# Softmax heads in pairs: value products in plain fp32 at two places of the array, turned blocks copied once

## The chip, the cores and the metric

One NeuronCore of a Trainium2 chip runs the whole program. The metric is the device time of one execution in microseconds (us). Engines are named as in the profile: PE (matrix multiply; PEld its weight loads), DVE (vector), ACT (activation), POOL (GpSimd) and SP (which only starts DMAs here). Each works through its own instructions in order and waits on semaphores for the others.

## What is computed

A decoder trunk of two layers over 1024 tokens of width 1024, all in float32. Layer 0 mixes tokens by stick-breaking attention, layer 1 by latent attention (12 heads in 6 pairs, 96 wide for queries and keys, 64 wide for values, causal). In each layer 4 memory heads attend to 256 memory rows without a mask. The change touches the softmax heads only, which compute, head by head:

```python
sc = jnp.einsum('bhqd,bhkd->bhqk', q_blk, k).astype(jnp.float32) * scale
sc = jnp.where(key_pos <= q_pos, sc, -jnp.inf)      # latent heads only
p = jax.nn.softmax(sc, axis=-1)
o = jnp.einsum('bhqk,bhkd->bhqd', p.astype(v.dtype), v)
```

## The kernel before, in words

The program runs in stages: memory heads, stick-breaking, output projection with SwiGLU, and the same again for layer 1 with latent_inputs and latent_heads in the place of stick-breaking. The matrices are multiplied as float32r, a form of fp32 that PE takes in one pass with rounded operands. To keep precision an operand is split into a rounded upper part (hi, made by ACT) and the rest (lo, made by DVE or POOL), and two or three products are added up (`product3`, L82 to L84).

**Attend** (from L764) is the softmax attention of both the memory heads and the latent heads. A job is one head and one half of the queries (512 of them, four tiles of 128). Its steps are written into one list that all engines walk:

- S: the scores of one tile of 128 queries into one of two score buffers (PE), and the negated maximum of the rows (DVE, L931). S waits until the exponentials of the tile two before are done.
- P: the exponentials with their sum (ACT, L906). I and R: the reciprocal and the scaling of the rows (DVE, L937, L943).
- T: one block of 128 keys is turned by up to four transposes into a bank (PE, L882), which ACT copies as the upper part (L914) and from which DVE subtracts it for the lower (L948).
- V: the value product of the block turned one T earlier. The stationary operand `self.values(h, j)` is 128 wide: 64 columns of the upper and 64 of the lower part of the values. It is multiplied with the upper (L891) and the lower part (L893) of the turned block, so the bank holds two halves of 64 partitions.
- E: ACT copies the second half (L920), DVE adds the first (L954), and SP stores 64 x 512 numbers.
- X: extra work that the caller puts at certain places.

A causal job of half 0 has 4 blocks of 512, 384, 256 and 128 columns; one of half 1 has four of 512 and then the same four, 8 in all. The list has one slot for each T. In a slot the order is: missing R and I, T, V of the block before (and E), P, S as far as `plan` says, X as `extras` says.

**latent_heads** runs a loop of 5 turns over pairs of heads, between a prologue and a last pair (`closing`, without extras and without the next pair's scores). A turn attends for pair g and prepares pair g+1 by extras, all through one bank (7): eight projections ("project", each 24 matmuls), their statistics ("sum", "root", "normalise", "rotate" on ACT, DVE and POOL), the hi and lo parts of the weights after ("next weights": ACT; `lower_weights`: POOL, L2126), the split of the values (ACT L2192 and L2203, POOL L2121), and eight "turn" steps (four transposes of queries or keys, L2297; ACT upper part, L2196; DVE lower part, L2254). The order on POOL is written out by hand in `prepare`: `rotate(0)`, `lower_weights`, `rotate(1)`, `lower_values(0)`. DVE's "rotate" step waits for two products of POOL (rot_pool) before it overwrites their input.

Of the kernel before, what the change touches and what calls it, by code (L numbers as in the profile page):

```python
# [6 lines left out]
P = 128  # L7
F32 = mybir.dt.float32
F32R = mybir.dt.float32r
# [758 lines left out]
class Attend:  # L768
# [4 lines left out]

    def __init__(self, nc, ctx, tag, mem, psum, k, jobs, keys_of, blocks_of, causal, scores, values, store,
                 rows_mem, ring, score_banks, out_banks=(6, 7), plan=None, extras={}):
        self.nc, self.k, self.jobs, self.causal, self.ring = nc, k, jobs, causal, ring
        self.keys_of, self.blocks_of, self.scores, self.values, self.store = keys_of, blocks_of, scores, values, store  # L780
        self.p = [[rows_mem(f"{tag}_p{n}_{i}", [P, keys_of(4 * jobs[n][1] + i)]) for i in range(4)] for n in range(ring)]
        self.pt_hi = [mem(f"{tag}_pt_hi{s}", [P, HALF], F32R) for s in range(2)]
        self.pt_lo = [mem(f"{tag}_pt_lo{s}", [P, HALF], F32R) for s in range(2)]
        self.nmx, self.rsum, self.rinv = (mem(f"{tag}_{n}", [P, 4]) for n in ("nmx", "rsum", "rinv"))
        self.o_tmp = mem(f"{tag}_o_tmp", [HD, HALF])
        self.o_out = [mem(f"{tag}_o_out{s}", [HD, HALF]) for s in range(2)]
# [3 lines left out]
        (self.scores_made, self.nmax_done, self.exp_done, self.inv_done, self.rows_done,  # L790
         self.turned, self.hi_done, self.split_done, self.pv_made, self.tmp_done, self.out_done) = (
            ctx.semaphore(f"{tag}_{n}") for n in (
                "scores_made", "nmax_done", "exp_done", "inv_done", "rows_done", "turned",
                "hi_done", "split_done", "pv_made", "tmp_done", "out_done"))
        self.stored = [ctx.semaphore(f"{tag}_stored{s}") for s in range(2)]
        self.ns, self.nj = 4 * len(jobs), len(jobs)
        self.first = [sum(blocks_of(half) for _, half in jobs[:n]) for n in range(len(jobs) + 1)]
        self.nt = self.first[-1]

        if plan is None:
            plan = [6] + [min(self.ns, 4 * n + 6 + 4 * (j + 1) // blocks_of(half)) for n, (h, half) in enumerate(jobs)
                          for j in range(blocks_of(half))]
# [33 lines left out]
        for n in range(self.nj):  # L839
            blocks = blocks_of(jobs[n][1])  # L840
            for j in range(blocks):
                tau = self.first[n] + j
                row_up_to(max(rows, 4 * n + 4))
                inverse_up_to(exps - 1)
                steps.append(("T", n, j, tau))
                if tau:
                    steps.append(("V",) + self.of(tau - 1))
                    if j == 0:
                        steps.append(("E", n - 1))
                exp_up_to(made)  # L850
                score_up_to(plan[tau + 1])
                steps += [("X", x) for x in extras.get(tau, ())]
        steps += [("V",) + self.of(self.nt - 1), ("E", self.nj - 1)]
        row_up_to(plan[-1])
        self.steps = steps

        self.closing = [s for s in steps if s[0] not in "SPIR" or s[1] < self.nj]

    def of(self, tau):

        n = max(m for m in range(self.nj) if self.first[m] <= tau)
        return n, tau - self.first[n], tau

    def columns(self, n, j):

        return max(0, j - 4 * self.jobs[n][1]) * P if self.causal else 0

    def pe(self, pe, steps, turn=0, extra=None):
        for kind, *step in steps:
            if kind == "S":  # L870
                n, i = step
                s, (h, half) = 4 * n + i, self.jobs[n % self.nj]
# [3 lines left out]
            elif kind == "T":  # L876
                n, j, tau = step
                pe.wait_ge(self.rows_done, turn * self.ns + 4 * n + 4)
                if tau >= 2:
                    pe.wait_ge(self.split_done, turn * self.nt + tau - 1)  # L880
                for i in range(self.columns(n, j) // P, 4):
                    last = pe.transpose(self.t_ps[tau % 2][:, i * P:(i + 1) * P],  # L882
                                        self.p[n % self.ring][i][:, j * P:(j + 1) * P], self.k["ident"][:])
                last.then_inc(self.turned, 1)
            elif kind == "V":
                n, j, tau = step
                c0, h, o = self.columns(n, j), self.jobs[n][0], self.o_ps[n % len(self.o_ps)]
                pe.wait_ge(self.split_done, turn * self.nt + tau + 1)
                if j == 0:
                    pe.wait_ge(self.out_done, 1 + turn * self.nj + max(n + 1 - len(self.o_ps), 0))  # L890
                pe.matmul(o[:, c0:HALF], self.values(h, j), self.pt_hi[tau % 2][:, c0:HALF],  # L891
                          start=j == 0, stop=False, skip_group_check=True)
                pe.matmul(o[:, c0:HALF], self.values(h, j), self.pt_lo[tau % 2][:, c0:HALF], start=False,  # L893
                          stop=tau + 1 == self.first[n + 1], skip_group_check=True).then_inc(self.pv_made, 1)
            elif kind == "X" and extra:
                extra(pe, step[0], turn)

# [61 lines left out]
    def begin(self, sp):  # L959

        for s in (self.pv_made, self.out_done):
            sp.sem_inc(s, 1)
# [1432 lines left out]
```

## Time and profile before

| what | us |
|---|---|
| runs | 3103.78, 3103.95, 3100.43 (median 3103.78) |
| profiled execution | 3095.97 |
| its span | 3094.2 |
| PE busy in it | 2708.3 |
| stretch of the memory heads' attention, layer 0 and layer 1 | about 113 to 160, 1580 to 1628 |
| latent_heads: prologue, five loop turns, last pair | 1784 to 1849, 1849 to 2219.6, to 2279 |

A row of a group of instructions has busy time and mean duration, then the idle time before it and what ended that. In a timeline a row is one instruction or a run of them; the bracket is the idle time just before it. The start of a matmul is recorded, its end is modelled, so how long a matmul holds the array is read from the distance between starts.

### The profile page before, as it was taken

Reading aid. Unit: us, or ns where it says so; the run is one execution under the profiler, and the core shown is the slowest. Engines: PE = TensorE matmul, PEld = TensorE weight load, DVE = VectorE, ACT = ScalarE, POOL = GpSimd, SP = SyncE. Lnnn points to the kernel's source line nnn. Section 1 sums busy time; section 2 is a strip of 40 time slices with the busy share of each in tenths; the row PEclk is TensorE's granted clock in tenths of the full one; section 3 lists DMA queues with packets and bytes.
Section 4 is the critical chain, followed back from the end, with each engine's and each line's share of the span. In section 5 each row is a group of like instructions: output and inputs, shape, how many; then the busy total and the mean of one; then the engine's idle time right before and its main releaser. Section 6 shows DMA issues by size and latency. Waiting matters only on the chain. (4 is left out here: it accounts for less than half of the span.)

```text
span 3094.2 us, 40579 instructions
## 1 busy us (share of the span) xinstructions
PE 2708.3 (88%) x13104; PEld 2239.9 (72%) x13104; DVE 1479.6 (48%) x2548; ACT 1296.6 (42%) x2794; POOL 1036.7 (34%) x722
## 2 busy tenths in 40 slices
PE   5679999879899998999567668888879899998999
PEld 4567777657688886888547657777757688886887
DVE  5636666652855553111562236666643755553111
ACT  4435555652433332222442236666643433332222
POOL 2034445550544442444102011111120544443443
PEclk9899999999999999999788868999989899999999
DMA  3020000042222223454202000000041222223454
GB/s 110 11 65 28 28 27 27 7 147 92 69 81 82 83 82 133 143 170 138 67 11 60 12 23 6 20 22 24 7 170 68 82 81 81 81 81 123 151 171 139
DMA packets 143097, 232.38 MB, mean 75 GB/s; under 512 B 17056, under 2 KB 93856, under 8 KB 143008
## 3 DMA queue, kind: packets, MB, share of 16 engines
q1 hardware_dynamic: 143008, 231.24, 22.5%
q8 instruction: 50, 0.82, 0.1%
q14 instruction: 39, 0.32, 0.0%
HBM read 182.98 MB, written 48.23 MB: 75 GB/s over the span
## 5 line engine op out<-in xcount | busy, mean ns | idle before, releaser
L1485 POOL TENSOR_TENSOR l0s_run_lo<-l0s_run,l0s_run_hi 128x512 fp32r<-128x512 f32 (+3 forms) x144 | 177.4, 1232 | 219.2 <-DVE l0s_run_hi L1652 218.5
L363 POOL TENSOR_TENSOR l1f_dn_lo<-l1f_dn_raw,l1f_dn_hi 128x1024 fp32r<-128x1024 f32 x44 | 106.1, 2412 | 141.9 <-ACT l1f_dn_hi L428 141.9
L363 POOL TENSOR_TENSOR l0f_dn_lo<-l0f_dn_raw,l0f_dn_hi 128x1024 fp32r<-128x1024 f32 x44 | 105.7, 2403 | 140.3 <-ACT l0f_dn_hi L428 140.3
L82 PE MATMUL banks<-ht_hi,l0s_w_hi 128*128 128x512 f32 x288 | 140.3, 487 | 12.7 <-POOL l0s_w_lo L1475 12.7
L82 PE MATMUL banks<-l1f_dn_hi,l1f_a_hi 128*128 128x512 f32 x352 | 138.0, 392 | 15.3 <-issue 12.6
L82 PE MATMUL banks<-l0f_dn_hi,l0f_a_hi 128*128 128x512 f32 x352 | 138.2, 393 | 12.7 <-issue 11.8
L82 PE MATMUL banks<-l1f_T_hi,l1f_op_hi 128*128 128x512 f32 x352 | 139.6, 397 | 10.1 <-ACT l1f_b L444 5.3
L82 PE MATMUL banks<-l0f_T_hi,l0f_op_hi 128*128 128x512 f32 x352 | 139.1, 395 | 10.1 <-ACT l0f_b L444 5.3
L1642 DVE SCALAR_TENSOR_TENSOR l0s_run<-banks,l0s_soft 128x512 f32<-128x512 f32 (+3 forms) x144 | 80.2, 557 | 135.8 <-ACT l0s_soft L1543 134.7
L84 PE MATMUL banks<-l1f_T_hi,l1f_op_lo 128*128 128x512 f32 x352 | 139.3, 396 | 0.0
L83 PE MATMUL banks<-l1f_T_lo,l1f_op_hi 128*128 128x512 f32 x352 | 139.1, 395 | 0.0
L84 PE MATMUL banks<-l0f_T_hi,l0f_op_lo 128*128 128x512 f32 x352 | 138.9, 395 | 0.0
L83 PE MATMUL banks<-l0f_T_lo,l0f_op_hi 128*128 128x512 f32 x352 | 138.5, 394 | 0.0
L83 PE MATMUL banks<-l0f_dn_lo,l0f_a_hi 128*128 128x512 f32 x352 | 138.0, 392 | 0.0
L84 PE MATMUL banks<-l0f_dn_hi,l0f_a_lo 128*128 128x512 f32 x352 | 137.8, 391 | 0.0
L83 PE MATMUL banks<-l1f_dn_lo,l1f_a_hi 128*128 128x512 f32 x352 | 137.6, 391 | 0.0
L84 PE MATMUL banks<-l1f_dn_hi,l1f_a_lo 128*128 128x512 f32 x352 | 137.5, 391 | 0.0
L948 DVE TENSOR_TENSOR l1aa_pt_lo<-banks,l1aa_pt_hi 128x512 fp32r<-128x512 f32 (+2 forms) x144 | 79.3, 550 | 116.1 <-ACT l1aa_pt_hi L914 115.9
L589 DVE TENSOR_TENSOR l1f_a_lo<-l1f_a_raw,l1f_a_hi 128x512 fp32r<-128x512 f32 x44 | 33.9, 770 | 208.0 <-ACT l1f_a_hi L426 208.0
L1514 ACT ACTIVATE l0s_soft<-banks 128x512 f32<-128x512 f32 (+3 forms) x144 | 70.9, 492 | 147.6 <-PE banks L1710 101.5
L589 DVE TENSOR_TENSOR l0f_a_lo<-l0f_a_raw,l0f_a_hi 128x512 fp32r<-128x512 f32 x44 | 32.2, 732 | 207.7 <-ACT l0f_a_hi L426 207.7
L1758 PE MATMUL banks<-l0s_wt,l0s_v 128*128 128x512 f32 (+3 forms) x288 | 119.0, 495 | 9.3 <-DVE l0s_o_out L1663 7.5
(481 smaller groups left out, 8600.3 us busy)
## 6 DMA issues: line engine op xcount, KB each, us to landing
l0f_raw<-in_w_ffn_gu_dram SPq DMA_DIRECT2D x22, 1024.0 KB, 5.2
l0f_dn_raw<-in_w_ffn_down_dram SPq DMA_DIRECT2D x44, 512.0 KB, 3.9
l1f_raw<-in_w_ffn_gu_dram SPq DMA_DIRECT2D x22, 1024.0 KB, 5.2
l1f_dn_raw<-in_w_ffn_down_dram SPq DMA_DIRECT2D x44, 512.0 KB, 4.0
hidden_rows<-l0f_hid SPq DMA_DIRECT2D x22, 512.0 KB, 2.8
l0f_a_raw<-hidden_rows SPq DMA_DIRECT2D x44, 256.0 KB, 3.1
hidden_rows<-l1f_hid SPq DMA_DIRECT2D x22, 512.0 KB, 2.7
l1f_a_raw<-hidden_rows SPq DMA_DIRECT2D x44, 256.0 KB, 3.1
```

The costliest lines, as they stand in the source:

```text
L82: pe.matmul(out, l_hi, r_hi, start=first, stop=False, skip_group_check=True)
L83: pe.matmul(out, l_hi, r_lo, start=False, stop=False, skip_group_check=True)
L84: return pe.matmul(out, l_lo, r_hi, start=False, stop=last, skip_group_check=True)
L363: pool.tensor_tensor(dn_lo[e][:], dn_raw[e][:], as_f32(dn_hi[e][:]), ALU.subtract).then_inc(dn_lo_done, 1)
L589: dve.tensor_tensor(a_lo[e][:], a_raw[e][:], as_f32(a_hi[e][:]), ALU.subtract).then_inc(a_lo_done, 1)
L948: dve.tensor_tensor(self.pt_lo[tau % 2][:, c0:HALF], self.t_ps[tau % 2][:, c0:HALF], as_f32(self.pt_hi[tau % 2][:, c0:HALF]), ALU.subtract ...
L1485: pool.tensor_tensor(run_lo[t % NR][:, f:HALF], run[t % NR][:, f:HALF], as_f32(run_hi[t % NR][:, f:HALF]), ALU.subtract).then_inc(run_spli ...
L1514: act.activation(s[:, f:HALF], psum[b % NZ][:, f:HALF], ACT.Abs).then_inc(abs_done, 1)
L1642: dve.scalar_tensor_tensor(r[:, f:HALF], psum[t % NZ][:, f:HALF], 0.0, soft[t % NA][:, f:HALF], ALU.max, ALU.add).then_inc(sp_done, 1)
L1758: pe.matmul(out_bank[:, f:HALF], v[:, j, h, :], wt[b % NW][:, f:HALF], start=bb in START, stop=bb in END, skip_group_check=True).then_inc( ...
```

## The change

Heads go two at a time. A job is now a pair of heads and a half of the queries (2 instead of 4 jobs in latent_heads, 4 instead of 8 in the memory heads). There is one T per head and block as before (so as many slots: 24 a turn), but one V per pair and block, in the slot of the next block's first head. Both T are plain fp32: ACT copies head 0's block, DVE head 1's. The value product is one fp32 matmul per head, 64 stationary columns, to partitions 0 to 63 and 64 to 127 of one bank. DVE copies the 128 x 512 result once and SP stores it once. The values are no longer split: in the memory heads they are read from `k32`; in latent_heads POOL copies them by a multiplication with one (`copy_values`). Extras, plan and the order of the turns are new, and waits on the turns at the head of the loop become waits before each part's first scores (`ready`).

```diff
@@ Attend.__init__, the list of steps
-        for n in range(self.nj):
-            blocks = blocks_of(jobs[n][1])
-            for j in range(blocks):
-                tau = self.first[n] + j
-                row_up_to(max(rows, 4 * n + 4))
...
+        for m in range(self.nj):
+            for j in range(blocks_of(jobs[m][1])):
+                u = self.first[m] + j
+                for h in range(2):
+                    row_up_to(max(rows, 4 * (2 * m + h) + 4))
+                    inverse_up_to(exps - 1)
+                    steps.append(("T", m, j, h, u))
+                    if h == 0 and u:
+                        steps.append(("V",) + self.of(u - 1))
+                        if j == 0:
+                            steps.append(("E", m - 1))
+                    exp_up_to(made)
+                    score_up_to(plan[2 * u + h + 1])
+                    steps += [("X", x) for x in extras.get(2 * u + h, ())]
@@ Attend.pe, V
-                pe.matmul(o[:, c0:HALF], self.values(h, j), self.pt_hi[tau % 2][:, c0:HALF],
-                          start=j == 0, stop=False, skip_group_check=True)
-                pe.matmul(o[:, c0:HALF], self.values(h, j), self.pt_lo[tau % 2][:, c0:HALF], start=False,
-                          stop=tau + 1 == self.first[n + 1], skip_group_check=True).then_inc(self.pv_made, 1)
+                for h in range(2):
+                    pe.wait_ge(self.copied[h], turn * self.nu + u + 1)
...
+                for h in range(2):
+                    last = pe.matmul(o[h * HD:(h + 1) * HD, c0:HALF], self.values(2 * pair + h, j),
+                                     self.pt[u % 2][h][:, c0:HALF], start=j == 0, stop=u + 1 == self.first[m + 1],
+                                     skip_group_check=True)
+                last.then_inc(self.pv_made, 1)
@@ Attend.act and Attend.dve, T
+                act.activation(self.pt[u % 2][0][:, c0:HALF], self.t_ps[0][:, c0:HALF],
+                               ACT.Copy).then_inc(self.copied[0], 1)
+                dve.tensor_copy(self.pt[u % 2][1][:, c0:HALF], self.t_ps[1][:, c0:HALF]).then_inc(self.copied[1], 1)
@@ Attend.dve, E
-                dve.tensor_tensor(self.o_out[n % 2][:], self.o_ps[n % len(self.o_ps)][0:HD, :], self.o_tmp[:],
-                                  ALU.add).then_inc(self.out_done, 1)
+                dve.tensor_copy(self.o_out[m % 2][:], self.o_ps[m % len(self.o_ps)][:]).then_inc(self.out_done, 1)
@@ Attend.begin
+        sp.sem_inc(self.pv_made, self.nu)
@@ latent_heads
-    turns = [(a, h, half) for h in range(2) for half in range(2) for a in range(2)]
+    turns = [(a, h, half) for half in range(2) for h in range(2) for a in range(2)]
...
-    extras = {0: ["values 1", "project 0"], 1: ["project 1"], 2: ["project 2"], 3: ["project 3"],
-              4: ["project 4", "sum 0", "root 0"], 5: ["project 5", "normalise 0"], 6: ["project 6", "rotate 0"],
-              7: ["project 7"], 8: ["next weights", "sum 1", "root 1"], 9: ["normalise 1"],
-              10: ["rotate 1", "turn 0"], 11: ["used 1", "turn 1"], 12: ["turn 2"], 13: ["values 0", "turn 3"],
-              14: ["turn 4"], 16: ["turn 5"], 18: ["turn 6"], 21: ["turn 7"]}
-    plan = [8, 9, 10, 11, 12, 13, 13, 14, 14, 15, 15, 16, 16, 16, 17, 18, 19, 20, 20, 21, 21, 22, 22, 23, 24]
+    extras = {0: ["project 0"], 1: ["project 1"], 3: ["project 2"], 4: ["project 3"], 5: ["sum 0", "root 0"],
+              6: ["normalise 0", "project 4"], 7: ["rotate 0"], 8: ["project 5"], 9: ["turn 0"],
+              10: ["turn 1", "project 6"], 11: ["turn 2"], 12: ["turn 3", "project 7"],
+              13: ["next weights", "sum 1", "root 1"], 14: ["normalise 1"], 15: ["rotate 1"], 17: ["turn 4"],
+              18: ["turn 5"], 19: ["turn 6"], 20: ["turn 7"]}
+    plan = [8] + list(range(9, 17)) + [16] * 5 + list(range(17, 25)) + [24] * 3
...
+        def ready(pe, n, g):
+            pe.wait_ge(t_split, 1 + 8 * g + 2 * n + 2)
@@ POOL in latent_heads
-                pool.tensor_tensor(v[:, h, :, HD:], v_head(h), as_f32(v[:, h, :, 0:HD]), ALU.subtract).then_inc(v_split, 1)
+            def copy_values(n, g):
+                pool.wait_ge(evicted, 1 + NS * g + NS // 2 * (n + 1))
+                pool.wait_ge(at_.pv_made, at_.nu * g + (8, 12)[n])
+                pool.tensor_tensor(v[:, group(n), :], v32[:, group(n), :],
+                                   one[:].unsqueeze(2).broadcast_to([P, G // 2, HD]), ALU.mult).then_inc(v_copied, 1)
...
             def prepare(g):
                 rotate(0, g)
+                copy_values(0, g)
                 lower_weights(g + 1)
                 rotate(1, g)
-                lower_values(0, 2 * g)
+                copy_values(1, g)
```

## Rows read from the trace of the kernel before

**Rows 1.** The page, part 1: busy time, share of the span, instructions.

```profile
PE 2708.3 (88%) x13104; PEld 2239.9 (72%) x13104; DVE 1479.6 (48%) x2548; ACT 1296.6 (42%) x2794; POOL 1036.7 (34%) x722
```

**Rows 2.** Busy time by stretch: length, PE, PEld, DVE, ACT, POOL, clock, DMA.

```profile
112.00:160.00 48.00, 31.85 (x148) 21.99 (x148) 36.62 (x107) 27.49 (x80) 0.00 (x0) 0.89 0.10 21
...
1849.00:1923.30 74.30, 64.69 (x405) 58.61 (x404) 43.86 (x91) 49.79 (x161) 13.62 (x12) 0.84 0.03 7
...
2145.50:2219.60 74.10, 62.49 (x432) 55.46 (x432) 47.48 (x99) 52.00 (x167) 13.70 (x12) 0.98 0.07 19
2219.60:2279.00 59.40, 43.42 (x228) 34.55 (x228) 37.91 (x78) 28.36 (x62) 1.49 (x1) 0.91 0.05 11
```

**Rows 3.** Waits of PE, 1850 to 2280 us: total, times, longest.

```profile
PE banks L891 <- DVE l1aa_pt_lo L948: 44.0, 47, 3.4
PE banks L2297 <- DVE l1a_kt_lo L2254: 7.3, 8, 1.2
...
PE banks L891 <- DVE l1aa_o_out L954: 3.4, 3, 2.2
```

**Rows 4.** Waits of PE, last loop turn, 2143 to 2214 us.

```profile
PE banks L891 <- DVE l1aa_pt_lo L948: 7.2, 7, 3.4
```

**Rows 5.** Timeline of PE, last loop turn: start, duration, operation, idle before.

```profile
2192.96 0.39 PE L893 MATMUL banks<-l1aa_pt_lo,l1a_v 128*128 128x512 f32 x1
2193.19 0.39 PE L82 MATMUL banks<-l1a_kt_hi,l1a_qt_hi 96*128 96x512 f32 x1
...
2200.44 0.63 PE L82 MATMUL banks<-l1a_kt_hi,l1a_qt_hi 96*128 96x512 f32 x1
2200.87 0.63 PE L83 MATMUL banks<-l1a_kt_lo,l1a_qt_hi 96*128 96x512 f32 x1
...
2206.55 0.60 PE L882 MATMUL banks<-ident,l1aa_p 128*128 128x128 f32 x4
2206.91 0.31 PE L891 MATMUL banks<-l1aa_pt_hi,l1a_v 128*128 128x128 f32 x1
```

**Rows 6.** Timeline of PE in stick_breaking: one fp32 value product, 512 columns.

```profile
402.28 1.02 PE L1758 MATMUL banks<-l0s_wt,l0s_v 128*128 128x512 f32 x2
...
403.37 0.40 PE L83 MATMUL banks<-ht_lo,l0s_w_hi 128*128 128x512 f32 x1
```

**Rows 7.** Timeline of ACT after the last projection of a turn.

```profile
2192.49 0.33 ACT L2176 ACTIVATE l1a_q<-banks 128x192 f32<-128x192 f32 x1 [0.56 <-PE banks L84]
...
2196.39 1.28 ACT L2188 ACT_TABLE_LOAD   x1
...
2198.59 0.31 ACT L2188 ACTIVATE l1a_std<-l1a_ss,eps 128x16 f32<-128x16 f32 x1 [0.92 <-DVE l1a_ss L2232]
```

**Rows 8.** Timeline of POOL in the same turn.

```profile
2195.92 2.62 POOL L2126 TENSOR_TENSOR l1a_wq_lo<-l1a_wq_raw,l1a_wq_hi 128x1152 fp32r<-128x1152 f32 x1 [5.58 <-ACT l1a_wq_hi L2160]
2198.50 1.26 POOL L2126 TENSOR_TENSOR l1a_wk_lo<-l1a_wk_raw,l1a_wk_hi 128x512 fp32r<-128x512 f32 x1
2200.11 1.39 POOL L2131 TENSOR_TENSOR l1a_k<-k_rot,l1a_rstd 128x256 f32<-128x256 f32 x1 [0.35 <-DVE l1a_rstd L2236]
2201.46 0.90 POOL L2136 TENSOR_TENSOR l1a_rc<-l1a_q,rope_tab 128x128 f32<-128x128 f32 x1
2202.33 0.45 POOL L2137 TENSOR_TENSOR l1a_rd<-l1a_q,rope_tab 128x128 f32<-128x128 f32 x1
2205.11 0.49 POOL L2140 TENSOR_TENSOR l1a_q<-l1a_rc,l1a_rd 128x128 f32<-128x128 f32 x1 [2.33 <-DVE l1a_rb L2246]
```

**Rows 9.** Timeline: two turned blocks in a row through the one bank.

```profile
1824.21 1.09 PE L2297 MATMUL banks<-ident,l1a_q 128*96 128x128 f32 x4 [1.56 <-DVE l1a_kt_lo L2254]
```

**Rows 10.** Instruction groups, 105 to 160 us (memory heads, layer 0).

```profile
L948 DVE TENSOR_TENSOR l0ma_pt_lo<-banks,l0ma_pt_hi 128x512 fp32r<-128x512 f32 x16 | 11.1, 691 | 6.7 <-ACT l0ma_pt_hi L914 6.7
```

**Rows 11.** Instructions of lines 1663 and 2121: duration ns min/median/max.

```profile
L1663 DVE COPY l0s_o_out<-banks x12: 672/682/690, 270.3 to 656.4; 128x512 f32<-128x512 f32 x12
...
L2121 POOL TENSOR_TENSOR l1a_v<-l1a_v,l1a_v x12: 1315/1493/2010, 1820.7 to 2235.5; 128x512 fp32r<-128x512 f32 x12
```

More of the change, by code:

```diff
@@ L871, in pe @@
                 n, i = step
-                s, (h, half) = 4 * n + i, self.jobs[n % self.nj]
+                s, (h, half) = 4 * n + i, self.parts[n % self.np]
+                if i == 0 and self.ready:
+                    self.ready(pe, n, turn)
                 if s >= len(self.s_ps):
@@ L876, in pe @@
             elif kind == "T":
-                n, j, tau = step
+                m, j, h, u = step
+                n = 2 * m + h
                 pe.wait_ge(self.rows_done, turn * self.ns + 4 * n + 4)
[L879 to L882, printed above, removed]
+                if u:
+                    pe.wait_ge(self.copied[h], turn * self.nu + u)
@@ L883, in pe @@
+                for i in range(self.columns(m, j) // P, 4):
+                    last = pe.transpose(self.t_ps[h][:, i * P:(i + 1) * P],
                                         self.p[n % self.ring][i][:, j * P:(j + 1) * P], self.k["ident"][:])
-                last.then_inc(self.turned, 1)
+                last.then_inc(self.turned[h], 1)
             elif kind == "V":
-                n, j, tau = step
-                c0, h, o = self.columns(n, j), self.jobs[n][0], self.o_ps[n % len(self.o_ps)]
@@ L966, in sync @@
     def sync(self, sp, turn=0):
[L967 to L969 removed]
+        for m, (pair, half) in enumerate(self.jobs):
+            sp.wait_ge(self.out_done, 1 + turn * self.nj + m + 1)
+            sp.dma_start(self.store(pair, half, turn), self.o_out[m % 2][:]).then_inc(self.stored[m % 2], 16)
     def finish(self, sp, turns=1):
@@ L2073, in latent_heads @@
[L2073 to L2078 removed]
+        sem = lambda n: ctx.semaphore(f"{tag}_{n}")
@@ L2093, in _ @@
             at_.begin(sp)
-            for s in (made, evicted, squared, v_split, turned, t_split):
+            for s in (made, evicted, squared, t_split):
                 sp.sem_inc(s, 1)
+            sp.sem_inc(v_copied, 2)
+            sp.sem_inc(turned, 8)
             load(0)
@@ L2261, in _ @@
             with dve.Fori(0, PAIRS - 1) as g:
-                at_.dve(dve, at_.steps, g, lambda dve, step, g: step not in OWN and prepare(dve, step, g + 1))
+                at_.dve(dve, at_.steps, g, lambda dve, step, g: prepare(dve, step, g + 1))
             at_.dve(dve, at_.closing, PAIRS - 1)
```

218 lines of the change are left out of this document (92 added, 126 removed).

## The prediction

> **What bounds the kernel now.** I read the page's busy times first, then the busy times by stretch, then the waits of PE, then timelines. PE is busy 2708.3 of 3094.2 us [rows 1], but the change touches only three stretches, and each has its own limit.
>
> In a loop turn of the latent heads (five, 74.1 us each) PE is recorded busy 62.5 to 64.7 us, ACT 50 to 52, DVE 44 to 47 [rows 2]. PE is the limit, and its idle time is what an edit can win. Over all pairs it waits 44.0 us for the lower part of a turned block, 3.4 us for an output bank and, in the loop turns, two times about 7 us at the "turn" steps [rows 3]. The last turn alone has 7.2 us of waits of V, the longest 3.4 us [rows 4]. That one has a history: ACT, in order, first makes the next weights, loads a table (1.28 us), waits for DVE's sum and only then copies the block [rows 7]. After it PE runs for a while at half its clock, 1.2 and not 2.4 GHz: products of 512 columns start 0.43 us apart and not 0.23 [rows 5].
>
> In the last pair nothing but attention is left: 59.4 us, PE 43.4 busy, DVE 37.9 [rows 2]. The chain of scores, exponentials, turned block, hi, lo and product sets the pace. In the memory heads DVE is busy 36.6 of 48 us [rows 2], and its largest wait, 6.7 us, is for ACT's upper part [rows 10]: DVE and its partner bound that stretch.
>
> **The value products.** Before, a block of 512 columns costs two fp32r products of 0.23 us for each head [rows 5], so 0.93 us a pair. Summed over its blocks a head has 9 times 512 columns, which makes 8.4 us a turn. A plain fp32 product of 512 columns is recorded as two matmuls with a load each, and holds PE from 402.28 to about 403.14 (the second matmul after it starts at 403.37, and they run 0.23 apart): 0.86 us, two passes of 0.43 [rows 6]. No row shows two products at two column places. Bounds for a pair's block: 0.86 if both stream together, 1.72 if they don't. PE starts matmuls in order, here pass 1 and 2 of head 0, pass 1 and 2 of head 1. Pass 2 of a head needs its own place, pass 1 of the other head does not; so I take three steps of 0.43, the middle pair together: 1.29. A turn then costs 7.7, 11.6 or 15.5 us: -0.7, +3.2 or +7.1 (I take +3.2).
>
> By the Trainium skill, TensorEngine Tiling (Array Packing), "Theoretical Speedup" and "Key Properties", tiles work independently and two column tiles give up to twice the rate, but a change of tiling mode drains the engine. The first rule would make the pair 0.86 us and is a rival below; the second speaks against the change, since each V stands between full-width transposes and scores, two switches each, 24 a turn. No row here prices a switch, and the sum has none.
>
> **The waits of V.** The chain from a turned block to its product loses one of its two links: DVE's subtraction of 0.69 us behind ACT [rows 10], and head 0's copy has a slot to spare. Of the 7 us I leave 1. But the ACT backlog stays. From the start of the last eviction to the end of the root it needs 6.4 us (2192.49 to 2198.90), then it loads the table back (1.28) and makes the exponentials of score 16: some 8 us [rows 7]. PE has meanwhile the slots 13 to 15 up to score 18, which needs that buffer: three T at about 0.4 (0.36 to the next start [rows 5]), one V, two small S, about 3.3 us. So some 4.8 us of wait return at S. Net -1.4 us a turn.
>
> **POOL's queue, the term that decides.** `copy_values(0)` overwrites values that V 4 to 7 of the running pair read; it waits for pv_made of V 7. V 7 stands in slot 16. Behind it in POOL's queue stand `lower_weights` and `rotate(1)`. "rotate 1" is an extra of slot 15 on DVE and waits there for POOL's two products; "turn 4", slot 17 on PE, waits for the same chain. Before, the only wait on V in POOL's way was over in the turn's first slots ("values 1"): POOL goes from 2195.92 to 2202.8 through weights and rotation [rows 8], and PE never waited there. After V 7 POOL has: the copy, bounded by 1.3 and 2.0 from the subtraction of the same size [rows 11], taken as 1.4 since DVE stands still meanwhile; weights 2.62 + 1.26; rotation 1.39 + 0.90 + 0.45; the last addition 0.5 [rows 8]. Sum 8.5 us, 8.7 with hand-over. PE has in this time S 19 (three products of 0.23 and the mask, 0.76), T (0.4) and S 20 (0.4): 1.6. It stands still for 7.1 us. DVE stood too, so its maximum, rows and copy come late for V 8: 1 us more. Together +8.1. It can't be less than zero; at most, with the 2.01 copy, 9. PE's pause is longer than the one that ended at half clock, so I add 1 us for slow products behind it (a product of 512 columns loses 0.20 us there [rows 5]; I count five of them, in less dense work).
>
> **One bank, two uses in a slot.** Slots 10 and 12 hold a turn and a projection. A second use of bank 7 right behind a turn waits for ACT's and DVE's parts: 1.56 us [rows 9]. Two of these are 3.1 us, the other turns some 2, against the 3.0 now ((7.3 + 7.2) / 5, of which one row stands in [rows 3]). +2.1 us a turn.
>
> Loop turn: 3.2 - 1.4 + 8.1 + 1.0 + 2.1 = +13.0 us, times five = +65.
>
> **Last pair, prologue.** Without extras the POOL chain is gone. DVE and ACT lose about half their work on turned blocks. Of the 12.6 us of waits of V and bank there I take back some 60 percent and pay 1 to 3 for the products: -7 (between 0 and -12). In the prologue all eight turns stood behind "rotate 1"; now four go ahead of "project 7" (four times 2.65 us, 1.09 of transposes and 1.56 of wait [rows 9]) and four remain: +1. The values' split leaves ACT (1.3 us a turn) but PE isn't held by it: zero, covered by PE's own work; if that cover is gone it is a gain of at most 1 us a turn.
>
> **Memory heads.** For each pair and half DVE made four subtractions of 0.69 us and two additions about as long, and waited four times 0.4 for ACT (6.7 us over 16 [rows 10]). It now makes two block copies and one output copy of 0.68 (a copy from a bank is no cheaper than a subtraction [rows 11]). Three saved are 2.0 us, less some overlap 1.8, and waits 0.9: -2.7 for each of 4 units, in two layers, -21. Bounds: -26 if all DVE waits go, -12 if the products take 1.72 and hold up the scores. The dropped split of values: -1. The fewer and larger stores are nothing: SP is far from late; only the last store, some 2 us, is exposed as before.
>
> Sum: 65 - 7 + 1 - 21 - 1 = +37 us on the profiled execution's 3096.0, or 3133. The median of the runs is 7.8 us above it, so 3141 against 3103.8. A measurement of this kernel can tell about 0.2 percent, 6 us, from no change.
>
> **Rivals.**
> - **The two products stream wholly together.** 0.86 a block: 3.9 us a turn less (-19.5), memory -24, last pair -9: +12, 3116. For it: the places and banks allow it. Against: a product's two passes come before the other head's. Of this rival the Trainium skill's first rule above would be the reason. 14 percent.
> - **They don't overlap, so the change doesn't do what it says.** 1.72: +3.9 a turn (19.5), memory -14, last pair -4: +66, 3170. For it: every matmul in the trace starts only after the one before has streamed. 28 percent.
> - **POOL's wait is covered, and the shorter copy chain decides.** The place is slots 15 to 17: if ACT's backlog and late maxima hold PE back at score 18 as long as POOL needs, or V 7 comes earlier than I count, the 8.1 and 1.0 us of each turn go. 37 - 46 = -9, 3095; with products together 12 - 46 = -34, 3070. It decides once less than about 1 us of the 8.1 is left. Against: V 7 itself lies behind that backlog, so the two add up. 14 percent, around 3091.
> - My forecast has the remaining 44 percent, with its own range 3118 to 3160 from the bounds of last pair, memory heads and waits.
>
> Range: 3100 to 3178 leaves out most of the faster case and the upper edge of the serial one. Faster by over 0.2 percent only in the third rival (0.13); same where that one and the first meet (0.07); slower 0.80.
>
> **What would show it.** DVE's last subtraction of "rotate" waiting about 7 us for POOL once a turn, and PE's turn step after it idle as long; `copy_values` on POOL released by PE and followed without a gap by L2126's work; value products of a pair's block 1.29 us from first start to the next instruction; a loop turn of 87 us; the memory heads' stretch near 37 us. The forecast is wrong if a turn is under 76 us, or if POOL's copy starts when PE is not waiting soon after; serial if the next start is 1.72 behind.

## The result, and the profile after

The changed kernel takes 3137.0 us (median of 4 runs, 3133.2 to 3138.0) against 3103.9 for the kernel before, run beside it: a ratio of 1.0107, 95% interval 1.0089 to 1.0124. I forecast 3141, range 3100 to 3178. Each later group of runs had the kernel before beside it too (medians 3100.9 to 3103.6), so kernels are compared by their ratios; the changed kernel stands at 1.0107 x 3101 = 3134 on that scale.

The page, part 1, and the busy times by stretch (columns as in [rows 2]): the first layer's memory heads, two loop turns of the latent heads, and the latent prologue.

```profile
PE 2739.5 (87%) x13104; PEld 2217.7 (71%) x13104; DVE 1422.2 (45%) x2438; ACT 1226.6 (39%) x2652; POOL 1023.2 (33%) x723
```

```profile
105.00:153.30 48.30, 35.82 (x167) 21.70 (x165) 34.03 (x110) 23.11 (x74) 0.00 (x0) 0.85 0.05 17
1888.60:1973.80 85.20, 68.84 (x441) 53.81 (x440) 41.02 (x85) 44.26 (x154) 10.93 (x12) 0.90 0.05 17
2144.70:2230.00 85.30, 68.84 (x434) 53.90 (x434) 40.56 (x84) 43.63 (x150) 10.93 (x12) 0.90 0.05 16
...
1762.60:1840.80 78.20, 40.16 (x232) 35.70 (x232) 15.84 (x24) 24.34 (x104) 15.76 (x15) 0.67 0.12 33
```

DVE and ACT are relieved as intended (57 and 70 us over the whole run against [rows 1]), but PE is busy 31 us longer with the same 13104 matmuls. The five turns are best measured together, from the first transpose of the first pair's probabilities to that of the last pair. First before, then after:

```profile
1853.41 1.06 PE L882 MATMUL banks<-ident,l1aa_p 128*128 128x128 f32 x4
...
2231.79 0.62 PE L882 MATMUL banks<-ident,l1aa_p 128*128 128x128 f32 x4
```

```profile
1850.19 1.05 PE L875 MATMUL banks<-ident,l1aa_p 128*128 128x128 f32 x4
...
2278.29 0.66 PE L875 MATMUL banks<-ident,l1aa_p 128*128 128x128 f32 x4
```

Five turns: 378.4 before, 428.1 after, +49.7, or +9.9 a turn. (The 74.1 us from which I forecast was one turn of 73.8 to 77.8; the mean was 75.7.) PE's waits over all pairs after the change, to be read beside [rows 3]:

```profile
PE banks L2290 <- DVE l1a_q L2236: 23.4, 5, 5.5
PE banks L82 <- ACT l1aa_p L907: 22.1, 11, 3.8
PE banks L82 <- DVE l1a_kt_lo L2241: 15.6, 10, 1.6
PE banks L888 <- DVE l1aa_pt L943: 14.0, 20, 1.7
PE banks L875 <- DVE l1aa_p L938: 7.4, 6, 3.5
PE banks L2290 <- DVE l1a_kt_lo L2241: 3.0, 5, 0.6
PE banks L2290 <- DVE l1a_qt_lo L2241: 1.9, 5, 0.4
```

With two small ones that are not shown (1.3 and 1.1) these make 89.8 us; before, the rows of [rows 3] with one of 7.2 for turned blocks and two small ones made 63.1: +26.7. In the whole attention of the latent heads PE was busy 369.5 us and is now 385.6: +16.1. Together +42.8; that stretch grew from 436.6 to 478.7 us. So the waits of V fell (47.4 to 15.1), and three new ones cost more: turn 4 for the rotation, scores for exponentials, projections for the bank.

**The POOL chain** is there as forecast. POOL in the last loop turn:

```profile
2172.41 1.04 POOL L2118 TENSOR_TENSOR l1a_v<-l1a_v,l1a_one 128x512 f32<-128x512 f32 x1 [31.59 <-PE banks L888]
2173.41 2.62 POOL L2124 TENSOR_TENSOR l1a_wq_lo<-l1a_wq_raw,l1a_wq_hi 128x1152 fp32r<-128x1152 f32 x1
2175.99 1.26 POOL L2124 TENSOR_TENSOR l1a_wk_lo<-l1a_wk_raw,l1a_wk_hi 128x512 fp32r<-128x512 f32 x1
2177.21 0.61 POOL L2129 TENSOR_TENSOR l1a_k<-k_rot,l1a_rstd 128x256 f32<-128x256 f32 x1
```

And PE beside it, score 18 (waiting for ACT), V 7, and turn 4 (waiting for POOL's rotation through DVE):

```profile
2168.12 0.69 PE L82 MATMUL banks<-l1a_kt_hi,l1a_qt_hi 96*128 96x384 f32 x1 [3.63 <-ACT l1aa_p L907]
...
2170.34 1.98 PE L888 MATMUL banks<-l1aa_pt,l1a_v 128*64 128x512 f32 x4
...
2179.57 1.06 PE L2290 MATMUL banks<-ident,l1a_q 128*96 128x128 f32 x4 [4.35 <-DVE l1a_q L2236]
```

POOL stands idle for 31.59 us until V 7 is through, then copies, lowers the weights and rotates without a gap. DVE waits 8.2 us for it, PE 4.35.

### The profile page after: what moved, and what is told of

Same layout as the page of the kernel before. It is cut to its first block and busy times, and to the rows that moved or that the text cites. A ratio compares the mean times of both kernels' runs of the same rounds, so it can differ in the third digit from the quotient of the medians.

```text
span 3136.0 us, 40078 instructions
## 1 busy us (share of the span) xinstructions
PE 2739.5 (87%) x13104; PEld 2217.7 (71%) x13104; DVE 1422.2 (45%) x2438; ACT 1226.6 (39%) x2652; POOL 1023.2 (33%) x723
## 5 line engine op out<-in xcount | busy, mean ns | idle before, releaser
L82 PE MATMUL banks<-ht_hi,l0s_w_hi 128*128 128x512 f32 x288 | 141.2, 490 | 11.7 <-POOL l0s_w_lo L1463 11.7
L82 PE MATMUL banks<-l1f_dn_hi,l1f_a_hi 128*128 128x512 f32 x352 | 138.0, 392 | 14.1 <-issue 11.8
L358 POOL TENSOR_TENSOR l1f_hid<-l1f_c,l1f_gate 128x512 f32<-128x512 f32 x44 | 66.8, 1519 | 173.2 <-DVE l1f_c L550 173.2
```

Source lines behind the costliest of these rows:

```text
L82: pe.matmul(out, l_hi, r_hi, start=first, stop=False, skip_group_check=True)
L358: pool.tensor_tensor(hidden(q), cs[q][:], gate[q][:], ALU.mult).then_inc(hid_done, 1)
```

## The experiments

Twelve kernels ran; kernel 7, for example, is that of experiment 7. Ratios are to the kernel before.

**1. POOL's order.** On POOL alone:

```
-                copy_values(0, g)
                 lower_weights(g + 1)
                 rotate(1, g)
+                copy_values(0, g)
```

> The changed kernel with one edit: on POOL copy_values(0) stands behind rotate(1) and no longer ahead of lower_weights. My theory: the place of that copy, and nothing in the rotation itself, holds PE at turn 4 (4.4 us in the last turn). The wait of DVE's last rotate subtraction for POOL (8.2 us) falls under 2 us, PE's wait at turn 4 falls under 1 us, and the half-clock stretch behind it goes: a loop turn of 85.2 us becomes 78 to 81, the median 3137 becomes 3102 to 3115. Rival 1: another wait stands behind this one (ACT's backlog or the bank), turn 4 comes as late as before: within 5 us of 3137. Rival 2: only the 4.4 us of the row go and nothing with them: 3137 - 22 = 3115.

3100.1 us, 0.9996 (0.9987 to 1.0005), 2 us below my range: 34 us of the changed kernel's loss are gone, all that set it apart from the kernel before. DVE's wait for POOL and PE's at turn 4 have left the tables. PE's remaining waits over all pairs:

```profile
PE banks L82 <- ACT l1aa_p L907: 21.8, 11, 3.8
PE banks L82 <- DVE l1a_kt_lo L2241: 15.6, 10, 1.6
PE banks L888 <- DVE l1aa_pt L943: 14.0, 20, 1.7
PE banks L875 <- DVE l1aa_p L938: 7.5, 6, 3.5
```

Only the row of 23.4 us is missing; the others stand as they were. Yet 34 us went: PE's busy time over the pairs fell too, from 385.6 to 375.6, with the granted clock at 0.91 and not 0.89 of full. So the wait that POOL caused, 23.4 us, cost some 10 us more in slow products behind it. Both rivals fall.

**2 and 3. Do the two products run together?** Two kernels in which they can't, one with products over the full width of the array, one with both at one place of 64 columns. Both leave out the separation of the two heads' results; they serve for their times alone.

```
-                    last = pe.matmul(o[h * HD:(h + 1) * HD, c0:HALF], self.values(2 * pair + h, j),
...
+  full width:       last = pe.matmul(o[:, c0:HALF], v[:, 2 * j:2 * j + 2, :], ...
+  same place:       last = pe.matmul(o[0:HD, c0:HALF], self.values(2 * pair + h, j), ...
```

> The changed kernel, but in the latent heads each value product takes both heads' values (128 columns of the array) and writes the whole bank, so the two products can't stand side by side and there is no change of the array's shape. It leaves out the separation of the two heads. Theory A (side by side both products stream wholly together, and a block pays two changes of shape, 0.35 us): a pair's block of 512 columns costs 1.72 instead of 1.21, one of 128 columns 0.43 instead of 0.57; 15.5 us a turn instead of 11.9, six turns +21: 3158. Theory B (my prediction's three steps of 0.43, no price of a change of shape): every block a third dearer, 128 columns 0.43 instead of 0.32, 15.5 instead of 11.6: +23, 3160. The totals agree; the row of a 128-column block tells them apart. Theory C (they never ran together): no change, 3137.

> The changed kernel, but in the latent heads both heads' value products (64 columns each, as in the changed kernel) go to the same column place of the array and the same half of the bank. It leaves out the second head's own sum. Theory A (full overlap side by side, plus 0.35 us for two changes of shape): the overlap goes, the changes stay: 9 x 1.72 + 12 x 0.35 = 19.7 us a turn instead of 11.9, six turns +47: 3184. Theory B (three steps, a change of shape costs nothing): 15.5 instead of 11.6, +23: 3160, the same as the full-width kernel. Theory C (no overlap before): no change, 3137.

3144.9 us, 1.0140 (1.0124 to 1.0155), and 3164.5 us, 1.0219 (1.0195 to 1.0243): +10 and +35 us over the changed kernel. By their order they speak for theory A (B wants both alike, C neither dearer), but both are some 11 us short of its sums. The traces tell part of why. Three timelines of PE in the last pair, one block's products, the next eight transposes and the next block's products: the changed kernel, full width, same place.

```profile
2307.36 1.08 PE L888 MATMUL banks<-l1aa_pt,l1a_v 128*64 128x512 f32 x4 [0.44 <-DVE l1aa_pt L943]
2308.37 1.09 PE L875 MATMUL banks<-ident,l1aa_p 128*128 128x128 f32 x8
2309.90 0.65 PE L888 MATMUL banks<-l1aa_pt,l1a_v 128*64 128x512 f32 x2 [0.44 <-DVE l1aa_pt L943]
```

```profile
2307.04 1.96 PE L889 MATMUL banks<-l1aa_pt,l1a_v 128*128 128x512 f32 x4 [0.44 <-DVE l1aa_pt L944]
2308.83 1.04 PE L875 MATMUL banks<-ident,l1aa_p 128*128 128x128 f32 x8
2310.30 0.67 PE L889 MATMUL banks<-l1aa_pt,l1a_v 128*128 128x512 f32 x1 [0.44 <-DVE l1aa_pt L944]
```

```profile
2328.36 1.90 PE L889 MATMUL banks<-l1aa_pt,l1a_v 128*64 128x512 f32 x4 [0.44 <-DVE l1aa_pt L944]
...
2331.72 0.61 PE L889 MATMUL banks<-l1aa_pt,l1a_v 128*64 128x512 f32 x1 [0.44 <-DVE l1aa_pt L944]
```

All with the same idle 0.44 us in front, at the full clock. From block to block: 2.54, 3.26 and 3.36 us. Same place against full width, 0.10 us, I read as what going over to 64 columns and back costs; the two kernels differ besides only in the width of the weights loaded and of the output. Side by side against same place, 0.82 us, is the overlap: of two products of 0.86 us [rows 6] nearly one whole. The records say the same. In a block of the last loop turn the four matmuls start in two pairs (PE's timeline, two narrow windows):

```profile
2202.70 0.65 PE L888 MATMUL banks<-l1aa_pt,l1a_v 128*64 128x512 f32 x2
...
2203.18 0.60 PE L888 MATMUL banks<-l1aa_pt,l1a_v 128*64 128x512 f32 x2
```

The pairs start 0.48 apart. At one place no two of them start together (a block's four take 1.84 us to the next start in the third timeline, 0.46 each), so a pair is one matmul of each head: first passes together, then second passes. My expectations took 0.35 us for two changes of shape; that was the whole hand-over around a block, most of which a full-width product has too (1.79 us to the next start, of which two products stream 1.72).

With these prices full width should cost 9 x 0.82 - 12 x 0.10 = 6.2 us a turn, 37 in six turns, and same place 9 x 0.82 = 7.4, or 44. The runs gave 10 and 35. What is missing lies in PE's busy time (over the pairs 394.4 us with full width against 385.6, where the prices ask for 37 more), and with it in the clock. Windows of the third loop turn, of the same length and aligned on the turn's start, for full width, then the changed kernel, then same place:

```profile
2068.00:2089.00 21.00, 13.84 (x80) 9.94 (x78) 6.70 (x15) 10.49 (x27) 3.90 (x3) 1.00 0.00 0
```

```profile
2069.80:2090.80 21.00, 15.03 (x72) 11.41 (x72) 5.96 (x14) 9.29 (x25) 3.55 (x2) 0.76 0.00 0
```

```profile
2078.00:2099.00 21.00, 14.15 (x80) 9.11 (x78) 6.70 (x15) 10.06 (x27) 3.92 (x3) 1.00 0.00 0
```

With full-width products the granted clock stayed at 2.4 GHz (1.00) through the turn's first waits, where in the changed kernel it fell to 1.2 for a part (0.76). The waits are alike but not the same: two of 1.55 us before projections in each kernel, and at score 18 3.1 us with full width, 3.7 in the changed kernel, 3.0 at the same place. The third kernel shows that products of 64 columns are not by themselves what brings the clock down: with them, too, the window stands at 1.00, in this turn and the two after it, though not in the first two (0.84 in the second). What both kernels have in common is that the two heads' products follow each other. Why that left the clock higher stays open. Over the whole of the pairs the granted clock was 0.94 with full width, 0.91 at the same place and 0.89 in the changed kernel.

**4. The memory heads alone.** The changed memory heads with the latent heads of before (in code: the old Attend kept under another name for latent_heads).

> The kernel before with the change made in the two stretches of memory heads alone; the latent heads are those of before. My theory: what those stretches showed in the changed kernel is a gain of their own, 2 x 7.5 us, of which their prologues and the next stretch's start take back some 5: 3104 - 10 = 3094, ratio 0.997. Rival 1: the gain is wholly given back at the next stretch's start (a load or a first projection that is not earlier): 3104. Rival 2: it is the full 21 us of my prediction: 3083.

3086.7 us, 0.9952 (0.9938 to 0.9965): -15 us, between my theory and the full forecast. The part is a gain, and worth keeping alone. DVE's waits in the first layer's stretch of the changed kernel:

```profile
DVE l0ma_pt L943 <- PE banks L875: 5.3, 5, 3.2
DVE l0m_q_st L1194 <- PE banks L1279: 3.2, 2, 2.1
DVE l0ma_nmx L926 <- PE banks L1313: 2.8, 5, 1.6
DVE l0ma_o_out L948 <- PE banks L888: 2.5, 4, 1.3
```

The wait of 6.7 us for ACT [rows 10] is gone, but waits for PE took its place: in sum 13.0 us before, 14.9 now. The stretch went from 52.2 to 44.7 us, and DVE's busy time in it from 40.3 to 33.1: its saved instructions (4 x 2.0) came nearly in full, its saved waits didn't.

**5. The bank's second use.** The order of experiment 1, and the extras from slot 10 on spread out:

```
-              6: ["normalise 0", "project 4"], 7: ["rotate 0"], 8: ["project 5"], 9: ["turn 0"],
-              10: ["turn 1", "project 6"], 11: ["turn 2"], 12: ["turn 3", "project 7"],
-              13: ["next weights", "sum 1", "root 1"], 14: ["normalise 1"], 15: ["rotate 1"], 17: ["turn 4"],
-              18: ["turn 5"], 19: ["turn 6"], 20: ["turn 7"]}
+              6: ["normalise 0", "project 4"], 7: ["rotate 0"], 8: ["project 5"], 9: ["turn 0"], 10: ["turn 1"],
+              11: ["project 6"], 12: ["turn 2"], 13: ["turn 3"], 14: ["project 7"],
+              15: ["next weights", "sum 1", "root 1"], 16: ["normalise 1"], 17: ["rotate 1"], 19: ["turn 4"],
+              20: ["turn 5"], 21: ["turn 6"], 22: ["turn 7"]}
```

> The POOL order of the first experiment (3100), and the extras of the second half spread so that no slot holds a turn and a projection (project 6 in slot 11, turns 2 and 3 in 12 and 13, project 7 in 14, the rest one or two slots later). My theory: the 15.6 us that PE waits there ahead of projections for the lower part of a turned block (10 times 1.56) are paid because the second use stands right behind the first, and go: 3100 - 12 to 15 = 3085 to 3088, a loop turn near 75.5. Rival: the pace of that half is set by ACT's queue (evictions, exponentials), and the waits come up again at the scores: 3098 to 3102.

3105.1 us, 1.0013 (1.0004 to 1.0022): 5 us slower than experiment 1; my theory missed, and by more than the rival. Stretch of all pairs, experiment 1 and this one:

```profile
1836.40:2281.00 444.60, 375.64 (x2362) 293.32 (x2361) 235.62 (x483) 237.31 (x785) 60.84 (x60) 0.91 0.05 14
```

```profile
1833.50:2284.80 451.30, 383.75 (x2362) 301.51 (x2360) 235.77 (x483) 237.62 (x785) 62.22 (x60) 0.88 0.04 14
```

PE's waits sum to the same (65.7 and 64.9 us): 10 of the 15.6 us before projections went and came back at turns and scores. What grew is PE's busy time, by 8.1 us, with the clock at 0.88. Why these places suit the clock less I did not try.

**6. The prologue's order.** Experiment 1 with all projections ahead of all turns in the prologue, as before.

```
-                "project 4", "project 5", "turn 0", "turn 1", "project 6", "turn 2", "turn 3", "project 7",
-                "next weights", "sum 1", "root 1", "normalise 1", "rotate 1"] + [f"turn {n}" for n in range(4, 8)])
+                "project 4", "project 5", "project 6", "project 7", "next weights", "sum 1", "root 1", "normalise 1",
+                "rotate 1"] + [f"turn {n}" for n in range(8)])
```

> The POOL order of the first experiment (3100), and in the prologue of the latent heads alone the order of the kernel before (all projections, weights, second half of the rotation, then turns 0 to 7). My theory: the 6.4 us by which the prologue grew come from four turns in series ahead of project 7 and from projects 6 and 7 at half clock behind their waits, while turns 0 to 3 no longer stand behind a wait for the rotation anyway: from the first latent project to the first score 78.2 us becomes 72, the median 3094. Rival (my prediction's +1: the order costs almost nothing, the rest of the 6.4 lies in the earlier projects or loads): 77, 3099.

3093.1 us, 0.9972 (0.9963 to 0.9982): 7 us, as my theory said. The prologue's stretch is 71.8 us, as before, against 78.2. (These windows begin 11 us ahead of the first project; from that to the first score it is 58.7 against 65.1, the same 6.4.)

**7. Next weights later.** Kernel 5 with the edit below. The list for the prologue (`PREPARE`) gets the same order, "next weights" behind "rotate 1".

```
-              15: ["next weights", "sum 1", "root 1"], 16: ["normalise 1"], 17: ["rotate 1"], 19: ["turn 4"],
+              15: ["sum 1", "root 1"], 16: ["normalise 1"], 17: ["rotate 1"], 18: ["next weights"], 19: ["turn 4"],
...
-                lower_weights(g + 1)
                 rotate(1, g)
+                lower_weights(g + 1)
```

> The pooled and spread kernel, with next weights moved on ACT from slot 15 to slot 18, behind the root and the rotation, and lower_weights on POOL behind rotate(1). My theory: PE's wait of 3.8 us at score 18 is ACT's backlog (0.8 of copies and squares, 1.76 of upper weights, 1.28 table, 0.31 root, 0.58 block copy, 1.28 table), so taking 1.76 us out of it shortens it by as much in five turns, -9: 3077 to 3080. Rival: the wait is for DVE's sum and the tables, the weights fill time that ACT waits anyway: as the pooled and spread kernel, 3086.

3091.2 us, 0.9965 (0.9952 to 0.9979): -14 where -9 was expected; the time that I named, 3077 to 3080, started from 3086 for kernel 5 and so missed. PE's wait for exponentials fell from 24.3 to 16.4 us, near what I expected. The rest has two parts. PE's busy time over the pairs fell by 4.5 us (383.8 to 379.3) with the clock at 0.90 and not 0.88. And the edit reached the prologue, which my expectation left out: PE's wait at turn 4 there fell from 10.3 to 6.4 us, and from the first project to the first score it is 60.3 us and not 65.3.

**8. Opening scores first.** Experiment 7, and in the prologue turns 0 to 3 and the opening scores ahead of turns 4 to 7:

```
-            for step in PREPARE:
-                prepare(pe, step, 0)
+            for step in PREPARE[:20]:
+                prepare(pe, step, 0, BANK_USES[0])
             at_.pe(pe, at_.opening)
+            for step in PREPARE[20:]:
+                prepare(pe, step, 0, BANK_USES[0])
...
```

(PE's part; ACT and DVE walk the same order, and `PREPARE` is put into it.)

> The kernel with next weights late, and a prologue in which projections 4 to 7 stand together, turns 0 to 3 are made during the second half's rotation, and the opening scores, which need no more than turns 0 to 3, are made ahead of turns 4 to 7. My theory: the 10.3 us that PE waits at turn 4 in the prologue are filled, and projects 6 and 7 run at the full clock: -12 to -16 against the kernel with next weights late, so 3062 to 3067. Rival: the opening's exponentials and rows on ACT and DVE hold back the rotation and turns 4 to 7 by as much, only the order's 6 us come back: 3072.

3079.5 us, 0.9928 (0.9914 to 0.9942): -11.7 against kernel 7, just short of the 12 to 16 that I expected, and twice the rival's 6.

**9 and 10. Without the spreading.** Kernels 7 and 8 with the changed kernel's own slots (turn 1 with project 6, turn 3 with project 7), root in slot 13, next weights in 16:

```
...
+              10: ["turn 1", "project 6"], 11: ["turn 2"], 12: ["turn 3", "project 7"],
+              13: ["sum 1", "root 1"], 14: ["normalise 1"], 15: ["rotate 1"], 16: ["next weights"], 17: ["turn 4"],
...
```

> The slots of the changed kernel (turn 1 with project 6, turn 3 with project 7), the rotation first on POOL, and next weights on ACT at slot 16, behind the rotation. Theory A (the spread slots lost by the clock: they left PE's waits the same in sum, 65 us, and its granted clock at 0.88 of full and not 0.91): without the spreading the late weights give their 9 us (1.76 us of ACT ahead of score 18, five turns) on top of the first experiment's 3100, and the clock stays near 0.91: 3088 to 3092, no worse than the spread kernel with late weights (3091). Theory B (spreading was a gain that noise hid): 3096 to 3100.

> As the packed kernel with late weights, with the prologue that makes the opening scores ahead of turns 4 to 7. It gave 12 us in the spread kernel; if it adds, 3076 to 3080. Rival: the prologue's gain was that of the order of projections and turns alone (7 us): 3082 to 3085.

3096.2 us, 0.9980 (0.9970 to 0.9991), and 3081.8 us, 0.9931 (0.9912 to 0.9950). The first touches the lower edge of theory B's range, and its 12 runs reach from 3089 to 3102, over both ranges; it decides nothing between them. In its profiled execution the wait for exponentials is down from kernel 1's 21.8 us to 14.8, yet the way from the first transpose to the last product of the pairs is 434.4 us against 434.0: PE's busy time took the gain back (380.8 us in a stretch of 442.0, against 375.6 in 444.6). The second is 14 us below the first, so the opening adds here too, where the rival had 7; its time misses the 3076 to 3080 that I named, since it starts from 3096. It can't be told from kernel 8, and kernels 7 and 9 differ by 5 us with intervals that overlap. So spreading neither clearly wins nor clearly loses once the weights are late.

**11. Root early.** Kernel 10 with projects 6 and 7 in slots 9 and 10, sum and root in 11, normalise in 12, rotate in 13, while no score waits to be made:

```
-              6: ["normalise 0", "project 4"], 7: ["rotate 0"], 8: ["project 5"], 9: ["turn 0"],
-              10: ["turn 1", "project 6"], 11: ["turn 2"], 12: ["turn 3", "project 7"],
-              13: ["sum 1", "root 1"], 14: ["normalise 1"], 15: ["rotate 1"], 16: ["next weights"], 17: ["turn 4"],
+              6: ["normalise 0", "project 4"], 7: ["rotate 0"], 8: ["project 5"], 9: ["project 6"],
+              10: ["project 7"], 11: ["turn 0", "sum 1", "root 1"], 12: ["turn 1", "normalise 1"],
+              13: ["turn 2", "rotate 1"], 14: ["turn 3"], 16: ["next weights"], 17: ["turn 4"],
```

> As the packed kernel with the opening first, with projects 6 and 7 in slots 9 and 10, ahead of all turns, and sum 1 and root 1 in slot 11, normalise 1 in 12, rotate 1 in 13. Theory A (what PE waits for at score 18 is the root with its two table loads standing between scores 16 and 18 and their exponentials; in slot 11 no score stands behind them; and the 15.6 us of projections behind a turn go with them): -15 to -25: 3053 to 3063. Theory B (waits only move, as when the slots were spread, since ACT's evictions and the copies of a turned block stand behind each other there, and the clock falls behind three projections and short blocks): 3073 to 3080.

3056.2 us, 0.9850 (0.9832 to 0.9868): theory A. It is 26 us better than kernel 10 (whose own six runs lie up to 18 us apart), 1.5 percent under the kernel before, the best of the study.

**12. Root late again**, projections left early.

```
-              10: ["project 7"], 11: ["turn 0", "sum 1", "root 1"], 12: ["turn 1", "normalise 1"],
-              13: ["turn 2", "rotate 1"], 14: ["turn 3"], 16: ["next weights"], 17: ["turn 4"],
+              10: ["project 7"], 11: ["turn 0"], 12: ["turn 1"], 13: ["turn 2", "sum 1", "root 1"],
+              14: ["turn 3", "normalise 1"], 15: ["rotate 1"], 16: ["next weights"], 17: ["turn 4"],
```

> The fastest kernel so far (3056) with one part undone: sum 1 and root 1 back in slot 13, normalise 1 in 14, rotate 1 in 15; projects 6 and 7 stay in slots 9 and 10, ahead of all turns. Theory A (the root's two table loads stood ahead of the exponentials of scores 16 to 18): PE's wait there comes back, 2.2 us in each of five turns, and the half clock behind it with it: 3070 to 3080. Theory B (the gain came from the projections, which no longer follow a turn): 3054 to 3060, with PE's wait for exponentials still near 4 us in all. If both share: 3062 to 3068.

3072.8 us, 0.9905 (0.9889 to 0.9922): 17 of the 26 us come back, theory A. The other 9, which would be the projections', are not clear of the noise: this interval and kernel 10's (0.9912 to 0.9950) meet. The stretch of all pairs in kernels 10, 11 and 12:

```profile
1817.40:2267.90 450.50, 381.24 (x2378) 296.50 (x2376) 237.09 (x487) 241.77 (x791) 68.65 (x64) 0.90 0.05 16
```

```profile
1814.70:2235.30 420.60, 357.63 (x2378) 277.66 (x2376) 240.00 (x487) 242.11 (x791) 68.74 (x64) 0.95 0.05 17
```

```profile
1813.10:2254.40 441.30, 368.80 (x2378) 284.94 (x2376) 238.19 (x487) 242.40 (x791) 67.67 (x64) 0.92 0.05 16
```

And some of PE's waits in the same three, the largest among them:

```profile
PE banks L82 <- DVE l1a_kt_lo L2245: 15.5, 10, 1.6
PE banks L82 <- ACT l1aa_p L907: 14.6, 11, 2.2
PE banks L888 <- DVE l1aa_pt L943: 13.3, 18, 1.7
```

```profile
PE banks L888 <- DVE l1aa_pt L943: 16.1, 20, 1.7
...
PE banks L82 <- DVE l1a_kt_lo L2244: 8.4, 5, 1.7
...
PE banks L82 <- ACT l1aa_p L907: 3.6, 6, 0.6
```

```profile
PE banks L888 <- DVE l1aa_pt L943: 27.9, 20, 2.9
PE banks L82 <- ACT l1aa_p L907: 12.1, 11, 1.7
```

From 10 to 11 the stretch loses 29.9 us, and 23.6 of them are PE's busy time for the same instructions. In kernel 12 the root's two table loads stand ahead of exponentials again, and PE waits 8.5 us more for those and 11.8 more at V for DVE's copy than in kernel 11 (8 more at V when its waits for ACT's copy, 1.1 and 4.9 us, are counted too). With the root early none of these waits is over 1.7 us, and the clock is at 0.95. The 15.6 us before projections are gone in kernel 11; its row of 8.4 us is new, score 16 waiting for the keys of turn 3.

## Why the prediction was right

The time and the sign came out, and the deciding term was named in its right place. Most sizes did not hold, and that the sum came so near is in good part luck. Of the signs that I named, a loop turn took 85.6 us in the mean (I said 87), POOL's copy was released by PE and followed without a gap, and DVE's subtraction waited 8.2 us; but a pair's products took 1.01 us to the next start and not 1.29, and the memory heads' stretch shrank by 7.5 us, where I had said from 48 to near 37. The terms, by their order:

- **Value products, +3.2 a turn.** Failed step: "three steps of 0.43, the middle pair together". Both passes run together. A block of 512 takes 0.86 plus about 0.1 for the shape, which is the mechanism of the rival that I gave 14 percent; the whole to the next start is 1.01. I come to 9 x 0.86 + 12 x 0.1 = 8.9 against 8.4 a turn: +0.5, not +3.2. The Trainium skill, TensorEngine Tiling (Array Packing), "Theoretical Speedup" and "Key Properties", has both halves: column tiles up to twice the rate (0.82 of 0.86 us here), and a drain at a change of mode (here 0.10 us for going and coming back).
- **V's waits, -6, and 4.8 at score 18.** Right in kind: over all pairs 47.4 us before and 15.1 after, and new waits for exponentials of 22.1 us, at score 18 3.6 to 3.8 each where I said 4.8. In the last loop turn V's waits fell by 4.9 us and not by 6 (before, then after):

```profile
PE banks L891 <- DVE l1aa_pt_lo L948: 7.5, 8, 3.4
```

```profile
PE banks L888 <- DVE l1aa_pt L943: 2.6, 4, 1.7
```

- **POOL, +8.1.** Right place and cause, size too large: 23.4 us at turn 4 over five turns, 4.7 a turn, where I had 7.1. Two durations failed. From POOL's copy to turn 4 (2172.41 to 2179.57) it is 7.2 us and not 8.7: the copy took 1.04 us (in kernel 1, too, with DVE idle or busy beside it), and the rotation's first products 0.61 and 0.45 where I had taken 1.39 and 0.90 from [rows 8], made there with DVE's multiplications beside them. And PE had 7.2 - 4.35 = 2.8 us of work left and not 1.6, as it ran at 1.2 GHz behind its wait at score 18. The 1 us more for late rows was not POOL's: PE waits 7.4 us for rows over the six pairs (3.5 of them in the last), and 7.5 in kernel 1, where POOL's wait is gone.
- **Half clock, +1.** Failed, too small. Experiment 1 gives 34 us for the whole term, 23.4 of them waits; some 2 us a turn are clock. The sum POOL plus clock, 45.5 us in the forecast, measured 34.
- **Bank, +2.1.** By the waits of turns and projections: 15.6 + 3.0 + 1.9 + 1.3 against 15.4 before, +6.4 us or 1.3 a turn.
- **Loop turns together:** +65 forecast, +49.7 measured. The terms as measured (0.5, -4.9 and +4.3, 6.8, 1.3, and 0.8 for the late rows) make 8.8 of the 9.9 us a turn; what the last 1.1 are I can't say.
- **Last pair, -7.** From first transpose to the last product 42.7 us before, 40.1 after; the opening ahead of the first turn is 4.1 us shorter, which I had not priced: -6.7 together.
- **Prologue, +1.** Failed step: that four turns ahead of project 7 would only replace four behind it. Before, turns and projections did not alternate, so no projection paid the 1.56 us of [rows 9]; now turns 0 and 1 stand in front of project 6 and turns 2 and 3 in front of project 7. Each of the two waits 1.55 us and then runs mostly at half clock, 5.5 and 5.3 us where projects 1 to 5 take 3.0: +6.4 in all, and experiment 6 gives 7 back.
- **Memory heads, -21.** Failed step: "waits 0.9" saved for each unit. Measured -15 (experiment 4).

So 49.7 - 6.7 + 6.4 - 15 = +34, where the medians show 33. The forecast's +37 was this near because its errors met: the loop turns 15 us too dear (products 13 and POOL with its clock 11 too dear, other terms of the turn too cheap), against a prologue 5 and memory heads 6 us too cheap. The rival in which POOL's wait is covered is refuted by the wait itself, 23.4 us, and by what its removal gave in experiment 1; that in which the products don't overlap fell with experiments 2 and 3.

## What to carry to other kernels

Before moving a wait into an engine's queue, list what stands behind it there: one copy that had to wait for the middle of a pair held the rotation of the next, and moving one line won 34 us. Then look at a stretch's PE busy time beside its waits; when the waits stay and the busy time of the same instructions moves, look at the granted clock. Fewer and shorter pauses of PE gave back 10 us of busy time beside 23 us of waits in experiment 1, and 24 beside 6 in experiment 11. Put work that blocks ACT (a root with its table loads) where no score or product waits for ACT.

## What the hardware showed that I had not expected

- Two plain fp32 products at two column places run pass by pass together: 2.54 us from block to block against 3.36 at one place.
- In aligned stretches of 21 us with like waits the granted clock was 1.00 with full-width products and 0.76 in the changed kernel. It was 1.00, too, with 64 columns at one place in three of five turns, so the width alone doesn't explain it; the cause is open.
- POOL's product of 128x256 for the keys took 0.61 us with DVE idle and 1.39 in [rows 8], where DVE multiplied beside it (2200.06 to 2202.05). Its multiplication by one of 128x512 took 1.04 to 1.09 us in all 12 executions, with DVE idle or busy.
